# X times its norm weight goes into the layers' projections, and each token's norm factor is multiplied in at the evictions

## The chip, the core and the metric

The kernel runs on one core of a Trainium2 chip. The time is the device time of one execution in microseconds (us). TensorE is the matrix engine (its rows are marked PE, its weight loads PEld), VectorE is DVE, ScalarE is ACT, GpSimd is POOL, and SyncE (SP) issues the transfers. All of them run their own instruction streams in order and wait for each other through semaphores.

## What is computed

512 tokens of width 1024 go through a first block (a time mix, a state space part and a gated feed-forward), a norm, and then two hybrid layers. The end of the first block and the two layers are what the change touches:

```python
x = x + g_f * ffn                                  # end of the first block
x = rms_norm(x) * final_gain
for l in range(2):
    h = rms_norm_2(x, norm_g[l])                   # x * rsqrt(mean(x*x) + 1e-6) * g
    proj = h @ w_in[l]                             # latents, gates, conv, window q/k/v
    y = concat(mla(proj...) * silu(g_mla), conv(proj...) * silu(g_conv), swa(proj...) * silu(g_swa))
    x = x + y @ w_out[l]
```

In `mla`, the query and key-value latents are each normed over their own width before their second projection. The convolution multiplies two projections, filters the product over three tokens and multiplies by a third.

## The kernel before

Everything is held transposed: a tile is 128 features by 512 tokens, and X is eight such tiles. Each float32 product is done in three passes: an operand is split into a rounded high part and the remaining low part, and high times high, high times low and low times high are summed in PSUM. For the activations this split lies in H (`Hs[r]`, a pair for each of the eight row blocks of the input width). For the weights it is made as they arrive: the stream of 234 units of 512 KB each (eight 128x128 blocks) is loaded by SyncE into a ring of four, ScalarE writes the high part (L2151) and VectorE the low part (L1260). Each engine's program calls `blocks(n)` as TensorE consumes blocks, and at each new unit `ahead` puts the split of the next one into that engine's stream. The high and low parts have two places each, so a split waits until TensorE is done with the unit two before it.

All matmuls of one kind are issued by one helper (L394), all transposes by another (L397); VectorE's two-tensor operations are L1260, its scalar-tensor-tensor operations L1268, its copies L1271; ScalarE's activations are L2148 and its copies L2151; GpSimd's are L2790 and L2793. So rows are told apart by tiles, shapes and order.

PSUM banks are handed out in turn: `take` gives the bank that was freed longest ago and waits for the events that empty it; `give` puts it back with those events.

A layer starts with a norm. While the down projection (for layer 0) or the out projection (for layer 1) runs, VectorE adds each finished tile into X, ScalarE squares it and VectorE adds up the squares. After the last tile, TensorE sums the squares over the partitions (`token_sums`, one column per 128 tokens), VectorE and ScalarE make the reciprocal root of the mean for each token, VectorE writes it onto a diagonal (`diag`), and TensorE spreads it over all partitions by a product with ones (`spread`). For layer 0 two norms follow each other, the first block's last one (`f`) and the layer's own (`g`); the second is worked out from sums of squares that carry the first one's weight, so both spreads are made before any row. The two diagonals share one place in memory. Then VectorE makes the rows (`norm_two_rows`, `norm_apply`): X times weight times spread, for layer 0 first X itself and then the row. ScalarE copies the row as high part, and VectorE or GpSimd (in turn) subtracts for the low part. `dense_rows` multiplies row by row with the four latent tiles (three of 128 and one of 32 columns), so each row starts when its H is ready.

The latents are squared and copied by ScalarE, summed over the partitions by TensorE (24 matmuls of one column), and a small part is transposed. Then three stages follow, in which parts of several generators are woven by a fixed pattern, the same on all engines: `qk` (queries and keys by 128 tokens) with the gate tiles 4 to 7 of the projection, `heads` (scores, exponentials, products with V for eight heads) with the window's queries, keys, values and its gates (30 to 33) and the first convolution tiles, and `windows` (four windows of 128 tokens, in two rounds each of `windows` to one of the projection) with the rest of the convolution tiles. For each j of 0 to 3 the projection's order is 8+j, 16+j, 12+j, 20+j. Before, ScalarE copied 8+j to CH; VectorE multiplied 16+j with it into CU; GpSimd and VectorE applied the three taps; VectorE multiplied by 12+j; ScalarE copied 20+j to the gate tile. The round of windows 2 and 3 on VectorE is: tile 8+3, maxima of window 2, 16+3, scores of window 3, 12+3, maxima of window 3, 20+3. Softmax of a window needs VectorE's maxima, ScalarE's eight exponentials, VectorE's reciprocal and GpSimd's product, and only then TensorE's transposes.

## Time and profile before

| | |
|---|---|
| median of 3 runs | 1645.88 us (1645.59 to 1646.56) |
| the profiled execution | 1645.37 us, its span 1643.6 us |
| TensorE busy | 1492.7 us (91%) |
| VectorE busy | 805.6 us (49%) |
| ScalarE busy | 584.4 us (36%) |
| GpSimd busy | 269.5 us (16%) |
| mean granted TensorE clock | 0.959 |

The span is what the trace covers; the execution's time is 1.8 us longer. A granted clock of 1.00 is 2.4 GHz and 0.50 is 1.2 GHz. A row of the timeline gives the start, the duration, the engine, the line and operation, the output and inputs with their shapes, how many instructions are merged in it, and in brackets the idle time of that engine before it and who ended it. With merged instructions the duration is that of the whole group.

### The profile page before, as it was taken

The numbers are of one execution on the slowest core, as the hardware profiler recorded it, in microseconds if no ns is written. First come the engines' busy times: TensorE is split into PE (matmuls) and PEld (weight loads), VectorE is DVE, ScalarE is ACT, GpSimd is POOL, SyncE is SP. The second block draws the span as 40 slices with busy tenths as digits, with TensorE's granted clock in tenths as the row PEclk, the third lists the DMA queues.
The fourth block names the chain that finished last, engine by engine and source line by source line (L and its number), as shares of the span: only waits on it lengthen the run. The fifth ranks groups of instructions, "written<-read, shape, count | busy, mean of one in ns | idle before, by whom it ended". The sixth has DMA issues, their size and how long they took to land.

```text
span 1643.6 us, 23774 instructions
## 1 busy us (share of the span) xinstructions
PE 1492.7 (91%) x10032; PEld 1155.1 (70%) x10032; DVE 805.6 (49%) x1255; ACT 584.4 (36%) x1012; POOL 269.5 (16%) x225
## 2 busy tenths in 40 slices
PE   6998897987899999999988999988898899998899
PEld 3676675875688888888766777666676677766667
DVE  7766855245543323223445554356534655435652
ACT  4265231245333222322333434134523343323441
POOL 0000232001001101100012332222101233222210
PEclk9999999998899999999989999999998999999999
DMA  9258242521222232332311121201222112120121
GB/s 376 71 116 109 70 171 106 165 83 44 72 90 90 90 103 90 104 121 92 119 47 39 52 77 53 76 26 52 72 95 84 39 52 78 51 77 26 52 90 64
DMA packets 51369, 143.12 MB, mean 87 GB/s; under 512 B 13248, under 2 KB 17984, under 8 KB 50496
## 3 DMA queue, kind: packets, MB, share of 16 engines
q1 hardware_dynamic: 51264, 141.60, 27.2%
q8 instruction: 80, 1.31, 0.3%
q14 instruction: 25, 0.20, 0.0%
HBM read 136.90 MB, written 4.69 MB: 86 GB/s over the span
## 4 chain that ended last, share of the span: by engine, by line
PE 72%; DVE 12%; ACT 8%; issue 3%; POOL 1%; DMA 1%; SPq 1%; DVEq 0%; ACTq 0%
PE b L394 71%; ACT arena L2148 5%; DVE arena L1260 2%; DVE ring L1260 2%; DVE arena L1268 2%; PE b L397 1%; ACT ring L2151 1%; POOL arena L2793 1%; DVE arena L1978 1%; ACT L2148 1%; ACT arena L2151 1%; DVE X L1260 1%; DVE arena L2111 1%; ACT tile L2151 1%; DVE arena L1936 1%
## 5 line engine op out<-in xcount | busy, mean ns | idle before, releaser
L394 PE MATMUL b<-tile,ring 128*128 128x512 f32 x2288 | 702.4, 401 | 14.8 <-ACT tile L2151 7.7
L394 PE MATMUL b<-HR,ring 128*128 128x512 f32 (+1 forms) x1888 | 625.1, 407 | 62.9 <-DVE ring L1260 34.9
L394 PEld LDWEIGHTS b<-tile,ring 128*128 128x128 f32 x2288 | 435.1, 191 | 122.4 <-issue 14.3
L394 PEld LDWEIGHTS b<-HR,ring 128*128 128x128 f32 (+1 forms) x1888 | 363.1, 192 | 163.9 <-issue 61.6
L1260 DVE TENSOR_TENSOR ring<-ring,ring 128x1024 fp32r<-128x1024 f32 x186 | 254.8, 1372 | 298.6 <-ACT ring L2151 294.8
L2151 ACT ACTIVATE ring<-ring 128x1024 fp32r<-128x1024 f32 x186 | 195.6, 1054 | 210.2 <-PE b L394 210.2
L394 PE MATMUL b<-arena 64*64 64x64 f32 (+10 forms) x3104 | 232.2, 286 | 26.4 <-issue 9.7
L394 PEld LDWEIGHTS b<-arena 64*64 64x64 f32 (+5 forms) x3104 | 149.3, 149 | 98.1 <-issue 70.6
L1260 DVE TENSOR_TENSOR arena<-arena 128x512 f32<-128x512 f32 (+7 forms) x206 | 110.7, 569 | 74.8 <-ACT arena L2148 53.7
L2151 ACT ACTIVATE arena<-b 128x512 f32<-128x512 f32 (+2 forms) x146 | 78.2, 559 | 193.2 <-PE b L394 153.2
L2793 POOL TENSOR_SCALAR arena<-arena 128x128 f32<-128x128 f32 (+1 forms) x64 | 87.1, 1377 | 209.0 <-DVE arena L1983 209.0
L2790 POOL TENSOR_TENSOR tile<-arena,tile 128x512 fp32r<-128x512 f32 x38 | 51.1, 1351 | 427.9 <-ACT tile L2151 427.9
L2790 POOL TENSOR_TENSOR arena<-arena 128x256 f32<-128x256 f32 (+4 forms) x61 | 65.0, 1089 | 236.0 <-DVE arena L2120 88.3
L1260 DVE TENSOR_TENSOR arena<-b,arena 128x512 f32<-128x512 f32 (+3 forms) x78 | 47.8, 630 | 109.7 <-PE b L394 108.4
L2148 ACT ACTIVATE arena<-arena 128x256 f32<-128x256 f32 (+5 forms) x155 | 73.0, 493 | 78.2 <-DVE arena L1264 46.0
L2148 ACT ACTIVATE arena<-b,arena 128x512 f32<-128x512 f32 (+1 forms) x80 | 44.0, 559 | 112.7 <-DVE arena L1264 108.4
L2151 ACT ACTIVATE tile<-arena 128x512 fp32r<-128x512 f32 x58 | 35.2, 628 | 134.3 <-DVE arena L1260 115.4
L397 PEld LDWEIGHTS b<-cst,arena 128*128 128x128 f32 (+1 forms) x504 | 57.1, 138 | 19.7 <-issue 14.8
L397 PE MATMUL b<-cst,arena 128*128 128x128 f32 (+1 forms) x504 | 63.4, 276 | 7.8 <-POOL arena L2790 5.7
L394 PE MATMUL b<-ring,HR 128*128 128x512 f32 (+1 forms) x256 | 64.5, 344 | 1.7 <-DVE arena L1271 1.2
L2148 ACT ACTIVATE arena<-b,par 128x512 f32<-128x512 f32 (+1 forms) x62 | 40.3, 686 | 65.7 <-PE b L394 38.8
L2148 ACT ACTIVATE arena<-b 128x512 f32<-128x512 f32 (+1 forms) x44 | 24.7, 562 | 84.6 <-PE b L394 84.6
(117 smaller groups left out, 985.7 us busy)
## 6 DMA issues: line engine op xcount, KB each, us to landing
ring<-in_ws SPq DMA_DIRECT2D x218, 512.0 KB, 3.5
arena<-in_ws SPq DMA_DIRECT2D x15, 512.0 KB, 15.3
arena<-in_lw SPq DMA_DIRECT2D x2, 1280.0 KB, 5.5
X<-in_xT SPq DMA_DIRECT2D x2, 1024.0 KB, 6.3
arena<-scr_kpad SPq DMA_DIRECT2D x8, 256.0 KB, 11.5
X<-in_xT SPq DMA_DIRECT2D x1, 2048.0 KB, 8.0
outT<-X SPq DMA_DIRECT2D x8, 256.0 KB, 2.0
arena<-in_cst SPq DMA_DIRECT2D x1, 1088.0 KB, 5.0
```

The lines of the kernel that those rows point to most:

```text
L394: return self.e.matmul(out, lhsT, rhs, start=start, stop=stop, skip_group_check=True)
L397: return self.e.transpose(out, in_, self.k.C("ident"))
L1260: return self.e.tensor_tensor(out=out, in0=a, in1=b, op=op)
L1268: return self.e.scalar_tensor_tensor(out=out, in0=a, scalar=s, in1=b, op0=op0, op1=op1)
L1936: self.e.tensor_reduce(out=s_, in_=sq, op=ALU.add, axis=AX.X).then_inc(*dve.inc((l, "sums", q)))
L1978: self.e.tensor_reduce(out=mx[:, q:q + 1], in_=ps[:, o:o + n], op=ALU.max, axis=AX.X).then_inc(*dve.inc((l, "max", h, q)))
L2111: self.e.tensor_reduce(out=mx, in_=Z[:, :, lo:256], op=ALU.max, axis=AX.X).then_inc(*dve.inc((l, "wmax", n)))
L2148: return self.e.activation(out, a, f, scale=scale, **kw)
L2151: return self.e.activation(out, a, ACT.Copy)
L2790: return self.e.tensor_tensor(out=out, in0=a, in1=b, op=op)
L2793: return self.e.tensor_scalar(out=out, in0=a, scalar1=s1, scalar2=None, op0=op0)
```

## The change

H is no longer the normed row. For both layers it is X times the norm weight (for layer 0 times the product of both weights), without the token's factor, and is made tile by tile while the projection before it runs: `high` on ScalarE, `lower` on VectorE, all eight rows. GpSimd makes no low part of H any more. TensorE's latents follow the projection before them; `token_sums` comes between rows 3 and 4 and `spread` after row 7. The statistics are made on VectorE and ScalarE beside rows 4 to 7 (`token_factors`), and ScalarE copies the spreads to memory (`factors`). The latents are left unscaled, since their own norms take the factor out again if 1e-6 is divided by its square (`e2`). Everything else is multiplied by the factor as it is evicted: gate tiles and 8+j on VectorE instead of copies on ScalarE, the product with 16+j and that with 12+j by one further VectorE multiply each, the window's queries, keys and values by a per-token scalar in the evictions they had. The residual X of layer 0 gets the first block's last norm by eight VectorE products (`residual`), two after each of the gate tiles 4 to 7.

The diff, cut to its core (TensorE, then VectorE, then ScalarE):

```diff
@@ TensorE: latents, and its callers
-        self.norm_two()
         for l in range(2):
-            if l == 1:
-                self.norm("l1")
             self.layer(l)
...
+        self.dense_rows(tiles, ready, M, range(4))
+        for name in names:
+            self.token_sums(name)
+            self.give((name, "sums"), (nd, (name, "mean")))
+        self.dense_rows(tiles, ready, M, range(4, 8))
+        for name in names:
+            self.spread(name)
+            self.give((name, "spread"), (na, (name, "R")))
@@ VectorE
+    def lower(self, name, r, gain):
+        self.wait_ge(k.s("norm_act"), (name, "hi", r))
+        hi, lo = k.Hs[r]
+        self.stt(lo, k.Xk[r], gain, hi.bitcast(F32), ALU.mult, ALU.subtract).then_inc(*k.s("norm_dve").inc((name, "lo", r)))
...
+        if not l:
...
+            self.diag("f", "h2", r_)
+            self.wait_ge(act, ("g", "sqrt"))
+            self.e.reciprocal(r2, r2).then_inc(*dve.inc(("g", "root")))
+            self.wait_ge(dve, ("g", "root"))
+            self.tt(r2, r2, r_, ALU.mult).then_inc(*dve.inc(("g", "both")))
+            rt = r2
...
+        self.diag("l1" if l else "g", "g" if l else "f", rt)
+
+    def residual(self, r):
...
+        self.stt(X, X, k.pc("fgain", r), k.RF, ALU.mult, ALU.mult).then_inc(*k.s("norm_dve").inc(("f", "x", r)))
@@ VectorE, the end of the first block
             if n:
+                self.lower("g", n - 1, k.gg[:, n - 1:n])
                 self.add_square("f", n - 1)
                 self.add_square("g", n - 1)
         self.add_square("f", 7)
         self.add_square("g", 7)
+        self.lower("g", 7, k.gg[:, 7:8])
@@ VectorE, latents
-        self.dense_tiles(4, self.norm_apply("l1", [k.pc("ng1", r) for r in range(8)]) if l else self.norm_two_rows())
+        self.ahead()
+        for r in range(8):
+            self.blocks(4)
+            if r == 4:
+                self.token_factors(l)
@@ VectorE, dense_rest
+        def scaled(m, dst, event):
+            self.wait_ge(D, (name, m))
+            self.wait_ge(k.s("norm_act"), ("l1" if l else "g", "R"))
+            self.tt(dst, k.bank[name, m][:, :], k.RR, ALU.mult).then_inc(*dve.inc(event))
         for n in range(4):
             self.blocks(8)
+            scaled(4 + n, k.G[:, n, :], (l, "g", n))
+            if not l:
+                self.residual(2 * n)
+                self.residual(2 * n + 1)
             yield
...
         for j in range(4):
             self.blocks(8)
+            scaled(8 + j, k.CH, (l, "ch", j))
             yield
...
-            self.tt(CU[:, 2:514], k.bank[name, 16 + j][:, :], k.CH, ALU.mult).then_inc(*dve.inc((l, "cu", j)))
+            self.tt(CU[:, 2:514], k.bank[name, 16 + j][:, :], k.CH, ALU.mult).then_inc(*dve.inc((l, "cr", j)))
+            self.wait_ge(dve, (l, "cr", j))
+            self.tt(CU[:, 2:514], CU[:, 2:514], k.RR, ALU.mult).then_inc(*dve.inc((l, "cu", j)))
...
-            self.tt(y, y, k.bank[name, 12 + j][:, :], ALU.mult).then_inc(*dve.inc((l, "yc", j)))
+            self.tt(y, y, k.bank[name, 12 + j][:, :], ALU.mult).then_inc(*dve.inc((l, "yr", j)))
+            self.wait_ge(dve, (l, "yr", j))
+            self.tt(y, y, k.RR, ALU.mult).then_inc(*dve.inc((l, "yc", j)))
             yield
             self.blocks(8)
+            scaled(20 + j, k.G[:, 4 + j, :], (l, "g", 4 + j))
             yield
@@ ScalarE
+    def high(self, name, r, gain, *when):
...
+        self.af(k.Hs[r][0], k.Xk[r], ACT.Copy, scale=gain).then_inc(*k.s("norm_act").inc((name, "hi", r)))
+
+    def factors(self, name, dst):
...
+        self.wait_ge(k.s("norm_pe"), (name, "spread"))
+        self.cp(dst, k.bank[name, "spread"][:, :]).then_inc(*k.s("norm_act").inc((name, "R")))
@@ ScalarE, latents
+        if not l:
+            self.factors("f", k.RF)
+        self.factors("l1" if l else "g", k.RR)
         for n in range(3):
             ps = k.bank[name, n]
             self.wait_ge(D, (name, n))
```

## Rows read from the trace of the kernel before

**Rows 1.** The page's chain of work that ended last, share of the span by engine

```profile
PE 72%; DVE 12%; ACT 8%; issue 3%; POOL 1%; DMA 1%; SPq 1%; DVEq 0%; ACTq 0%
```

**Rows 2.** Windows: from:to, length, busy time of each engine, granted clock, DMA share

```profile
815.90:830.50 14.60, 6.39 (x32) 5.82 (x33) 9.03 (x18) 3.23 (x6) 2.14 (x4) 0.64 0.31 112
857.20:863.50 6.30, 6.30 (x15) 3.29 (x14) 0.30 (x2) 2.04 (x5) 0.61 (x1) 0.73 0.00 0
1269.00:1273.60 4.60, 4.60 (x15) 2.58 (x14) 0.31 (x2) 2.04 (x5) 0.61 (x1) 1.00 0.01 4
1082.80:1168.60 85.80, 71.94 (x332) 51.73 (x333) 53.01 (x72) 39.36 (x106) 19.89 (x9) 0.92 0.12 37
```

**Rows 3.** Timeline of TensorE at both layers' first projections

```profile
818.57 2.31 PE L394 MATMUL b<-cst,arena 128*128 128x1 f32 x16 [2.74 <-DVE arena L1260]
...
822.45 2.04 PE L394 MATMUL b<-nst,cst 128*128 128x128 f32 x8 [1.58 <-DVE nst L1416]
...
830.52 0.76 PE L394 MATMUL b<-HR,ring 128*128 128x512 f32 x1 [3.10 <-DVE tile L1260]
...
835.01 0.40 PE L394 MATMUL b<-tile,ring 128*128 128x512 f32 x1
...
837.79 0.39 PE L394 MATMUL b<-tile,ring 128*128 128x512 f32 x1
...
854.19 2.73 PE L394 MATMUL b<-cst,arena 128*128 128x1 f32 x24
...
1241.28 0.77 PE L394 MATMUL b<-HR,ring 128*128 128x512 f32 x1 [2.32 <-DVE tile L1260]
...
1265.98 2.73 PE L394 MATMUL b<-cst,arena 128*128 128x1 f32 x24
```

**Rows 4.** Timeline of VectorE at the same two boundaries

```profile
815.87 0.75 DVE L1268 SCALAR_TENSOR_TENSOR X<-b,ada,X 128x512 f32<-128x512 f32 x1 [3.23 <-PE b L394]
816.54 2.49 DVE L1260 TENSOR_TENSOR arena<-arena 128x512 f32<-128x512 f32 x4
818.94 1.22 DVE L1260 TENSOR_TENSOR ring<-ring,ring 128x1024 fp32r<-128x1024 f32 x1
...
1231.80 0.69 DVE L1260 TENSOR_TENSOR X<-b,X 128x512 f32<-128x512 f32 x1 [3.22 <-PE b L394]
```

**Rows 5.** Timeline of ScalarE, the first of the latents' squares in layer 0

```profile
852.31 0.60 ACT L2148 ACTIVATE arena<-b 128x512 f32<-128x512 f32 x1 [2.35 <-PE b L394]
```

**Rows 6.** Timelines of VectorE and TensorE in layer 0's query-key stage

```profile
873.22 1.75 DVE L1936 TENSOR_REDUCE arena<-arena 128x16 f32<-128x1536 f32 x1 [0.29 <-ACT arena L2148]
...
913.09 1.43 DVE L1264 TENSOR_SCALAR arena<-b,par 96x512 f32<-96x512 f32 x2
...
915.15 2.40 PE L394 MATMUL b<-arena 96*128 96x512 f32 x8 [0.97 <-ACT arena L2148]
```

**Rows 7.** TensorE's wait in layer 0's heads; VectorE's groups by shape, 1280 to 1640 us

```profile
1051.86 0.61 PE L394 MATMUL b<-HR,ring 128*128 128x512 f32 x1 [3.06 <-DVE ring L1260]
...
L1271 DVE COPY arena<-b 128x512 f32<-128x512 f32 x20 | 13.3, 679 | 6.8 <-PE b L394 6.6 <-PE b L397 0.2
...
L1260 DVE TENSOR_TENSOR arena<-b,arena 128x512 f32<-128x512 f32 x7 | 4.8, 681 | 7.4 <-PE b L394 7.4
```

**Rows 8.** Timelines of all engines in layer 0's window stage

```profile
1116.69 0.76 PE L394 MATMUL b<-HR,ring 128*128 128x512 f32 x1 [5.54 <-DVE ring L1260]
...
1119.99 2.27 DVE L2111 TENSOR_REDUCE arena<-arena 128x8 f32<-128x2048 f32 x1
...
1124.24 0.60 ACT L2151 ACTIVATE arena<-b 128x512 f32<-128x512 f32 x1 [9.57 <-PE b L394]
...
1129.39 3.61 POOL L2790 TENSOR_TENSOR arena<-arena 128x2048 f32<-128x2048 f32 x1 [13.93 <-DVE arena L2120]
...
1130.82 3.25 DVE L1260 TENSOR_TENSOR ring<-ring,ring 128x1024 fp32r<-128x1024 f32 x1 [0.35 <-ACT ring L2151]
...
1153.09 2.37 PE L397 MATMUL b<-cst,arena 128*128 128x128 f32 x16 [2.83 <-POOL arena L2790]
```

More of the change, by code:

```diff
@@ L1008, in latents @@
         pe, act, dve = k.s("lat_pe"), k.s("lat_act"), k.s("lat_dve")
[L1009 to L1012 removed]
+        na, nd = k.s("norm_act"), k.s("norm_dve")
+        names = ("l1",) if l else ("f", "g")
+        ready = [[(na, (names[-1], "hi", r)), (nd, (names[-1], "lo", r))] for r in range(8)]
+        tiles, M = [(self.name, n) for n in range(4)], [128, 128, 128, 32]
+        self.dense_rows(tiles, ready, M, range(4))
[6 more added lines that the diff above has]
+            self.give((name, "spread"), (na, (name, "R")))
         for n in range(3):
@@ L2031, in gate @@
             self.blocks(8)
[L2032 to L2033 removed]
+            scaled(30 + n, k.G[:, 8 + n, :], (l, "g", 8 + n))
         for n, _ in enumerate(self.window_norm(l)):
@@ L2583, in latents @@
         name = f"l{l}"
-        self.dense_tiles(4, self.norm_apply("l1") if l else self.norm_two_rows())
+        self.ahead()
+        for r in range(8):
+            self.blocks(4)
+            if r == 4 and l:
+                self.norm_root("l1", k.r_)
+            elif r == 4:
+                self.norm_root("f", k.r_)
+                self.norm_root("g", k.r2_)
+        if not l:
+            self.factors("f", k.RF)
+        self.factors("l1" if l else "g", k.RR)
         for n in range(3):
@@ L2704, in dense_rest @@
         for j in range(4):
-            self.blocks(8)
-            self.wait_ge(dve, (l, "cu", j - 1) if j else (l, "pad"))
-            copy(8 + j, k.CH, (l, "ch", j))
-            yield
-            self.blocks(8)
-            yield
-            self.blocks(8)
-            yield
-            self.blocks(8)
-            copy(20 + j, k.G[:, 4 + j, :], (l, "g", 4 + j))
-            yield
+            for _ in range(4):
+                self.blocks(8)
+                yield
         self.gates(l, range(4, 8))
```

186 lines of the change are left out of this document (81 added, 105 removed).

## The prediction, made before the changed kernel had run

> **What bounds the kernel now.** I read the chain that ended last first: 72% of it is TensorE and 12% VectorE [rows 1], so time is to be had only where TensorE stands still. Then the timeline of TensorE around the two layers' first projections. Between the last matmul of the down projection and the first of layer 0's latents lie 14.6 us, in which only small matmuls (column sums, spreads) run and the granted clock averages 0.64 [rows 2, 3]: TensorE waits for sums, roots, the spread, and then for the first row of H. In layer 1 the same gap is 9.5 us, from the last eviction into X to the first latent matmul [rows 3, 4]. That is what the change attacks. Third, I read what VectorE does where TensorE waits later in a layer, because the change moves work there: the stage with the window attention (1082.8 to 1168.6 us) has TensorE busy for 71.9 of 85.8 us [rows 2], and its waits end with a VectorE weight split or with a GpSimd product that VectorE started [rows 8]. VectorE has 53.0 us of work there, but it is a queue with long waits in it, so added work counts whenever it stands ahead of a split that TensorE wants.
>
> **The boundary.** The split of X times its weight is made per tile while the down (or out) projection runs, so the latents' rows 0 to 3 can follow at once. Twelve matmuls of 512 columns take 2.78 us (835.01 to 837.79), 96 take 22.2. The sums stay on TensorE, now between rows 3 and 4: 2.3 us for both in layer 0 [rows 3], half of that (1.0) in layer 1, with one. Does the second weight unit come in time? VectorE has after the last down tile: eviction 0.75, then four adds at 0.62 each, then the split 1.22, which began at 818.94 [rows 4]. Two more products (0.67 each) put it at 820.3, ready at 821.6; TensorE wants it 5.55 us after 815.9, at 821.4: 0.2 us lost. Layer 0's rows then end at 815.9 + 22.2 + 2.3 + 0.2 = 840.6 instead of 854.2; layer 1's at 1231.8 + 23.2 = 1255.0 instead of 1266.0 [rows 3, 4]. But the spreads now stand behind the rows and in front of the evictions: one took 2.04 us at the 1.2 GHz level [rows 3], so about 1.0 at 2.4 GHz. In layer 0: spread, the second diagonal on VectorE (0.69; it shares its memory with the first, so it waits), spread, and ScalarE's copy before the latents' squares (0.5; the squares are alike [rows 5]), with hand-overs 3.5 us; in layer 1 one spread and one copy, 1.6 us. Before, the first square began at 852.31, 1.9 us ahead of the rows' end [rows 5], because tile 0 was finished first. That lead is lost. So the first square starts at 844.1 instead of 852.3 (-8.2) and at 1256.6 instead of 1264.1 (-7.5). The 24 one-column matmuls behind it ran 2.73 us after the rows; now they follow each square and end 0.9 us after the third, which is 0.8 us sooner against the squares. Together **-9.0 and -8.3 us**. The statistics' own chain (root, reciprocals, four more tiny ones) lies under rows 4 to 7, 11 us.
>
> **The clock.** The stretch of one-column matmuls and the first product after it took 4.6 us at full clock in layer 1, and 6.3 us at 0.73 in layer 0 [rows 2]: the same work, and one of two such stretches cost 1.7 us. Afterwards each stretch holds more idle time (waits for diagonal, copy, squares), and layer 0 has one more in the middle of its rows, the sums. Bounds: nothing, and three falls (5.1 us). I take one and a half, **+2.6 us**, since layer 1's becomes emptier than the one that fell.
>
> **Query-key stage.** The gate tiles' evictions move from ScalarE (which waited for TensorE there anyway, so it frees nothing) to VectorE, in layer 0 with two residual products each: 0.65 + 2 x 0.75 us (the eviction into X has that form [rows 4]). Before the second reduction VectorE is idle 0.29 us in layer 0 [rows 6], and the other layer runs alike. That reduction sets when a bank is free for the next projection, so +1.8 and +0.35 us. The third and fourth reductions have over 3 us of idle time before them, which hides it. At the end of the stage the last group stands ahead of the transposed keys' eviction (913.09), and the scores wait at 915.15 for ScalarE, 0.7 us later than VectorE [rows 6]: +1.7 and +0.15. Together **+4.0**. If a slow clock falls on this stage, TensorE is late and hides 1.8 of it; that is the lower bound, 1.1 us for both layers with the rest.
>
> **Heads.** Evictions that only change from copy to product cost nothing I can find: a copy 128x512 out of PSUM takes 0.68 us and a product 0.68 [rows 7]. New are two products with the spread per convolution tile. Two of them lie ahead of a chain that ends in a split TensorE waits for: the wait of 3.06 us at 1051.86 [rows 7] is such a chain (product, GpSimd tap, two taps, masks, exponentials, split), +0.7 (a product and its hand-over). One round earlier such a chain shows no wait yet; it can cost from nothing to 0.7, and as the two rounds are alike but for a tap I take 0.5. Both layers: **+2.4**, bounds 0 and 3.
>
> **Windows.** Here a wait is added. At 1119.99 VectorE begins the maxima of window 2, while TensorE still runs projection tile 8+3, begun at 1116.69. The product that evicts this tile now comes first in VectorE's queue and waits for its end; behind it stand the maxima, the exponentials that depend on them, the reciprocal, GpSimd's product and the next weight splits. ScalarE had the same wait, for its copy at 1124.24, so the exponentials began half a us later, at 1124.7 [rows 8]. Step by step: the product on y before window 1 shifts all by 0.7. Eviction done at 1125.4, maxima 2.3 and small ones 0.5, exponentials from about 1128.2: +3.4. The split behind them lasts until GpSimd's product of 3.61 us ends (it took 3.25 us at 1130.82, 1.22 at 818.94 [rows 4, 8]). TensorE's tile 12+3 then starts 2.2 us late, 20+3 3 us late. Two more products (+1.35) stand before the exponentials of window 3; those are 4.7 us late, GpSimd's last product too, and for that TensorE waits at 1153.09 [rows 8]. So +4.6 per layer, **+9.2**. Bounds: 1.4 (only the first product counts) and 13 (each longer wait also lowers the clock).
>
> On that hold: splits beside a GpSimd product took 3.25 us against 1.22 alone [rows 4, 8]. The Trainium skill (SBUF — State Buffer, Who interferes with whom) says that a VectorE instruction with two SBUF inputs and a GpSimd instruction that reads SBUF exclude each other, the loser waiting for the whole instruction. By that rule the products with the spread, which have two SBUF inputs, would be held where GpSimd scales probabilities; I find none of these on TensorE's path, so the sum would stay.
>
> **Sum.** -17.3 + 2.6 + 4.0 + 2.4 + 9.2 = +0.9 us. The profiled execution took 1645.37 us (span 1643.6 and 1.8 around it), the median of the runs is 1645.88, 0.5 above it. 1645.9 + 0.9 = 1646.8 us.
>
> **Rivals.** *Faster:* the boundary pays and most of the later work stays hidden. That is so if VectorE's wait for tile 8+3 costs little (windows +1.4 a layer, 2.8) and the clock does not fall anew: -17.3 + 4.0 + 2.4 + 2.8 = -8, 1638 us. For it: VectorE is busy only 53.0 of 85.8 us in the worst stage. Against it: the queue order, which idle time elsewhere doesn't mend.
> *Slower:* the wait for tile 8+3, in the window stage, is the mechanism. It makes TensorE stand for 4.4 us instead of 2.8 ahead of 1153.09 and for 1.5 and 0.9 us at two tiles that had no wait. If these lower the clock once more in each layer (1.7 us each, as above) and the boundary's stretches fall all three times (+2.5 on my figure), it is +0.9 + 3.4 + 2.5 = +6.8, 1652.7 us. It decides from about 6 us a layer on, where my sum has 4.6.
> *The rows don't start at once:* if the first rows wait for the last tile's split (a unit or a bank not ready), some 5 us of each gap return: 1656 us. Against it: rows 0 to 3 need only tiles finished long before.
>
> **How the numbers follow.** A measurement of this kernel can tell 0.2% (3.3 us) from no change. Forecast 0.45, faster rival 0.24, slower 0.27, rows late 0.04. The forecast's own range is 1642.5 to 1650; the range that leaves out no more than 2 in 10 is 1639 to 1653. Of the forecast's chance nearly all lies within 0.2%; a little of each rival does too. So faster 0.24, same 0.46, slower 0.30.
>
> **What would show it.** Right: the first latent matmul within 0.3 us of the last down matmul and rows ending 24.7 us later; the first square 28 and 25 us after that boundary in layers 0 and 1; VectorE idle until the end of tile 8+3, with the maxima behind it, and the wait for GpSimd near 4.4 us; 4.6 us more from the first window score to the out projection. Wrong: if the stretch from the first latent product to the out projection is not longer by some 6 to 9 us a layer, the gain of the boundary stays and the kernel is faster; if rows 0 to 3 show waits for splits, the boundary's gain was too large.

## The result and the profile after

The changed kernel takes 1660.19 us (median of four runs, 1656.38 to 1665.68), the kernel before beside it 1646.22. The ratio is 1.0087, interval 1.0054 to 1.012: **slower**, by 14 us, where the forecast was 1646.8. The profiled execution is the quickest of the four, 1656.38 us (span 1654.6). The four runs differ by 9 us, and from the quickest to the slowest their mean granted clocks are 0.959, 0.958, 0.951 and 0.948. The four of the kernel before lie within 1.5 us of each other. One of the 17 runs of the kernel before that stood beside e9 to e12 below took 1898.4 us at a granted clock of 0.739 and enters none of the ratios and means.

First the new boundary, TensorE's timeline (start, duration, engine, line, operation, count, and in brackets the idle time before it with what ended it). These lines answer to [rows 3]:

```profile
822.09 0.47 PE L396 MATMUL b<-HR,ring 128*128 128x512 f32 x1 [0.22 <-issue]
...
827.72 1.84 PE L396 MATMUL b<-cst,arena 128*128 128x1 f32 x16
...
842.44 1.16 PE L396 MATMUL b<-nst,cst 128*128 128x128 f32 x8 [0.78 <-DVE nst L1255]
...
844.77 3.58 PE L396 MATMUL b<-cst,arena 128*128 128x1 f32 x24 [1.17 <-ACT arena L2182]
```

and the first of the latents' squares on ScalarE, which answers to [rows 5]:

```profile
844.13 0.59 ACT L2182 ACTIVATE arena<-b 128x512 f32<-128x512 f32 x1
```

The rows follow the down projection at once, with 0.22 us lost for the second weight unit (VectorE's split of it begins at 820.77 and takes 1.22 us). The column sums take 1.84 us in the middle. The first square starts at 844.13, where I had 844.1, and 8.2 us earlier than before [rows 5]. The boundary did what it should.

Then TensorE's waits in layer 0, where the change added work to VectorE. They answer to [rows 6, 7, 8]:

```profile
871.27 0.80 PE L396 MATMUL b<-HR,ring 128*128 128x512 f32 x1 [3.62 <-DVE arena L1255]
...
911.62 4.00 PE L396 MATMUL b<-arena 96*128 96x512 f32 x8 [1.76 <-DVE arena L1259]
...
1026.13 0.47 PE L396 MATMUL b<-HR,ring 128*128 128x512 f32 x1 [0.54 <-DVE ring L1255]
...
1052.55 0.76 PE L396 MATMUL b<-HR,ring 128*128 128x512 f32 x1 [3.78 <-DVE ring L1255]
...
1118.36 0.79 PE L396 MATMUL b<-HR,ring 128*128 128x512 f32 x1 [5.21 <-DVE arena L1255]
...
1139.55 0.47 PE L396 MATMUL b<-HR,ring 128*128 128x512 f32 x1 [1.66 <-DVE ring L1255]
...
1147.65 0.47 PE L396 MATMUL b<-HR,ring 128*128 128x512 f32 x1 [0.56 <-DVE ring L1255]
...
1159.88 3.65 PE L399 MATMUL b<-cst,arena 128*128 128x128 f32 x16 [4.57 <-POOL arena L2829]
```

Nearly every stall has the size that was forecast: 0.54 and 0.72 more in the heads (I had 0.5 and 0.7), 1.66 at tile 12+3 (1.5), 0.56 at tile 20+3 (0.9), 4.57 for GpSimd's last product (4.4). Only the one at 1118.36 is of another kind: it ends with a VectorE product that frees a bank (arena), and in [rows 8] it ended with a weight split (ring). The queues behind it, VectorE and then GpSimd:

```profile
1113.48 4.22 DVE L1255 TENSOR_TENSOR ring<-ring,ring 128x1024 fp32r<-128x1024 f32 x1 [0.54 <-ACT ring L2185]
1117.63 0.68 DVE L1255 TENSOR_TENSOR arena<-b,nst 128x512 f32<-128x512 f32 x1
...
1126.73 0.69 DVE L1255 TENSOR_TENSOR arena<-b,nst 128x512 f32<-128x512 f32 x1 [4.91 <-PE b L396]
1127.34 2.28 DVE L2145 TENSOR_REDUCE arena<-arena 128x8 f32<-128x2048 f32 x1
```

```profile
1113.02 3.60 POOL L2829 TENSOR_TENSOR arena<-arena 128x2048 f32<-128x2048 f32 x1 [12.22 <-DVE arena L2154]
1134.72 3.60 POOL L2829 TENSOR_TENSOR arena<-arena 128x2048 f32<-128x2048 f32 x1 [18.10 <-DVE arena L2154]
```

At 1126.73 stands the wait of the forecast: 4.91 us idle, the eviction of tile 8+3, and only then the maxima of window 2, which in [rows 8] began at 1119.99. At 1117.63 stands what I had missed: the eviction of tile 20+2 is behind a split of 4.22 us, and its bank is the one that tile 8+3 needs. The split began while GpSimd's product of 3.60 us was running and ended 1.08 us after it. The kernel before has this long split too, but there ScalarE evicted tile 20+2:

```profile
1112.32 4.22 DVE L1260 TENSOR_TENSOR ring<-ring,ring 128x1024 fp32r<-128x1024 f32 x1 [0.55 <-ACT ring L2151]
```

The Trainium skill (SBUF — State Buffer, Who interferes with whom) gives the rule for this pair, that the later one waits for the whole instruction; the trace agrees, with 1.22 us for the same split elsewhere [rows 4].

So where do 14 us come from? The stretches, cut at the same events in both profiles (last eviction of the down projection, first scores, last heads' products, first output rows past their split, and the same in layer 1):

| stretch | before, us | after, us | difference | forecast (without clock) |
|---|---|---|---|---|
| layer 0, boundary and query-key | 99.28 | 95.25 | -4.0 | -5.5 |
| layer 0, heads | 167.71 | 171.88 | +4.2 | +1.2 |
| layer 0, windows | 85.75 | 93.19 | +7.4 | +4.6 |
| output, boundary, query-key of layer 1 | 156.64 | 148.77 | -7.9 | -7.8 |
| layer 1, heads | 167.68 | 170.49 | +2.8 | +1.2 |
| layer 1, windows | 85.58 | 93.58 | +8.0 | +4.6 |
| sum of these | 762.64 | 773.16 | +10.5 | -1.7 |

The forecast's clock term of +2.6 lay in the first and fourth line. The same stretches of the changed kernel by windows (from:to, length, busy time and count of TensorE, its weight loads, VectorE, ScalarE, GpSimd, then granted clock, DMA share, GB/s); the third answers to the last of [rows 2]:

```profile
816.37:841.50 25.13, 24.91 (x120) 18.47 (x118) 10.26 (x21) 6.40 (x9) 3.15 (x4) 1.00 0.32 108
...
911.62:1083.50 171.88, 160.93 (x740) 123.15 (x741) 87.17 (x158) 55.68 (x116) 49.92 (x37) 0.97 0.19 62
1083.50:1176.69 93.19, 75.18 (x333) 54.67 (x333) 56.95 (x78) 37.81 (x103) 19.89 (x9) 0.89 0.10 34
...
1325.46:1495.95 170.49, 159.46 (x741) 122.29 (x741) 86.99 (x158) 56.39 (x116) 49.84 (x37) 0.98 0.19 64
1495.95:1589.53 93.58, 74.12 (x333) 53.66 (x333) 56.94 (x78) 37.81 (x103) 19.89 (x9) 0.89 0.11 34
```

The heads' 740 matmuls keep TensorE busy for 160.93 us; before it was 157.83 with the same count, at 0.99:

```profile
915.15:1082.86 167.71, 157.83 (x740) 121.19 (x741) 80.15 (x148) 58.41 (x119) 51.63 (x37) 0.99 0.19 65
```

The window stage has 75.18 against 71.94 [rows 2]. That is not waiting but slower work: the clock. Over the heads and windows of both layers TensorE's busy time grew by 8.9 us. Where it lies in the changed kernel, and where it lay before:

```profile
977.00:982.00 5.00, 5.00 (x16) 3.92 (x15) 3.01 (x3) 0.00 (x0) 4.13 (x3) 0.66 0.46 147
1103.00:1107.00 4.00, 4.00 (x12) 3.14 (x11) 3.97 (x6) 0.00 (x0) 0.00 (x0) 0.57 0.33 125
1117.00:1125.00 8.00, 6.64 (x18) 5.26 (x19) 4.83 (x7) 0.00 (x0) 0.00 (x0) 0.57 0.42 133
1158.00:1166.00 8.00, 6.12 (x26) 4.21 (x28) 4.71 (x4) 3.00 (x5) 1.74 (x1) 0.57 0.20 66
```

```profile
819.00:834.00 15.00, 9.44 (x39) 8.12 (x39) 8.66 (x18) 2.30 (x5) 3.43 (x5) 0.54 0.17 66
1236.00:1247.00 11.00, 7.77 (x22) 5.89 (x23) 6.64 (x10) 3.16 (x5) 2.51 (x2) 0.53 0.20 65
```

In a window with clock c, 2(1-c) of its length was at 1.2 GHz. Summed over windows of 1 us, the kernel before has 23.8 us at that level in its two boundaries, where TensorE had little to do, and 48.9 us in the rest of the two layers. The changed kernel has none in the boundaries and 78.4 us in the rest, nearly all of it next to waits of 1.8 to 6.8 us or to the squares behind the new boundary. Not every wait there is new: the low stretch at 977 follows a wait of 2.56 us that the kernel before has as well, without a fall. The two sums for the whole execution hardly differ (134 and 136 us). In the front part, which the change doesn't touch, each profile has 51 to 72 us, as it comes.

Two theories, then. **Queues:** what VectorE's order costs, some 11 us in the windows instead of 9.2, is the loss, and the clock is chance. **Clock:** the new stalls bring falls of the clock, onto busy matmuls. And within the second, either the falls follow the stalls, or an execution has its 136 us at 1.2 GHz whatever is done and the old boundary merely hid 24 of them.

### The profile page after: what moved, and what is told of

Its sections match the earlier page's. It is cut to its first block, busy times and chain, and to the rows that moved or that the text cites. A ratio compares the mean times of both kernels' runs of the same rounds, so it can differ in the third digit from the quotient of the medians.

```text
span 1654.6 us, 23782 instructions
## 1 busy us (share of the span) xinstructions
PE 1497.2 (90%) x10032; PEld 1157.4 (70%) x10032; DVE 823.9 (50%) x1297; ACT 573.9 (35%) x993; POOL 256.8 (16%) x217
## 4 chain that ended last, share of the span: by engine, by line
PE 70%; DVE 14%; ACT 7%; issue 4%; POOL 3%; DMA 1%; SPq 1%; DVEq 0%; ACTq 0%
PE b L396 69%; ACT arena L2182 4%; DVE arena L1255 3%; DVE arena L1263 2%; DVE ring L1255 1%; PE b L399 1%; DVE arena L1998 1%; ACT ring L2185 1%; POOL arena L2832 1%; POOL arena L2829 1%; DVE arena L2145 1%; DVE arena L1956 1%; DVE arena L1259 1%; DVE X L1255 1%; DMA arena<-scr_yd 1%
## 5 line engine op out<-in xcount | busy, mean ns | idle before, releaser
L396 PE MATMUL b<-arena 64*64 64x64 f32 (+10 forms) x3104 | 236.8, 287 | 28.8 <-issue 11.5
L2832 POOL TENSOR_SCALAR arena<-arena 128x128 f32<-128x128 f32 (+1 forms) x64 | 83.6, 1322 | 214.8 <-DVE arena L2003 214.8
L2185 ACT ACTIVATE arena<-b 128x512 f32<-128x512 f32 (+2 forms) x113 | 61.2, 563 | 97.4 <-PE b L396 58.6
L396 PE MATMUL b<-ring,HR 128*128 128x512 f32 (+1 forms) x256 | 64.8, 345 | 1.4 <-DVE arena L1266 1.2
L2182 ACT ACTIVATE arena<-b 128x512 f32<-128x512 f32 (+1 forms) x44 | 24.7, 562 | 115.6 <-PE b L396 115.6
```

The costliest lines, as they stand in the source:

```text
L396: return self.e.matmul(out, lhsT, rhs, start=start, stop=stop, skip_group_check=True)
L2182: return self.e.activation(out, a, f, scale=scale, **kw)
L2185: return self.e.activation(out, a, ACT.Copy)
L2832: return self.e.tensor_scalar(out=out, in0=a, scalar1=s1, scalar2=None, op0=op0)
```

## The experiments

All are compared with the kernel before, run beside them on the same chip (medians 1648.56, 1651.03 and 1650.34 us in the three groups, each on another chip, 1642.8 to 1656 in single runs). "At 1.2 GHz" is 2(1-clock) times the span, mean over the runs. Within each kernel's own runs, a microsecond more at that level goes with 0.31 us more time (all kernels pooled; 0.17 to 0.46 in single ones).

| run | what | median, us | ratio [95%] | at 1.2 GHz, us |
|---|---|---|---|---|
| kernel before (three groups) | | 1648.6 to 1651.0 | 1 | 138 to 142 |
| e5_after_again | the changed kernel | 1663.42 | 1.0088 [1.0069, 1.0106] | 163 |
| e1_no_factor | changed kernel, leaves the token factor out of gates and convolution | 1638.90 | 0.9936 [0.9919, 0.9953] | 133 |
| e2_late_ch | tile 8+3 evicted behind the maxima | 1652.37 | 1.0016 [1.0002, 1.003] | 142 |
| e3_no_second | changed kernel, leaves the second products out | 1647.17 | 0.9990 [0.9978, 1.0003] | 131 |
| e4_before_dve_evicts | kernel before, evictions on VectorE | 1659.61 | 1.0066 [1.0047, 1.0085] | 149 |
| e6_reordered | changed kernel, same work elsewhere | 1633.79 | 0.9913 [0.9896, 0.9930] | 120 |
| e7_after_filled | changed kernel, waits filled | 1647.98 | 0.9995 [0.9983, 1.0007] | 91 |
| e11_fill_one | changed kernel, one wait filled | 1653.17 | 1.0017 [1.0002, 1.0033] | 133 |
| e12_after_all_filled | e7 with one fill moved and one added | 1636.66 | 0.9921 [0.9900, 0.9941] | 78 |
| e8_before_filled | kernel before, boundary waits filled | 1643.08 | 0.9962 [0.9949, 0.9975] | 113 |
| e10_before_all_filled | kernel before, boundary and layer waits filled | 1629.36 | 0.9875 [0.9846, 0.9904] | 71 |
| e9_reordered_filled | e6, waits filled | 1621.12 | 0.9812 [0.9787, 0.9838] | 75 |

### The changed kernel again

> The changed kernel itself, beside the others on one chip. If the 9 us between its four runs are the clock's own spread, its median lies at 1656 to 1662 and its ratio to the kernel before at 1.005 to 1.009; put at the same time at 1.2 GHz as the kernel before (some 0.3 us of time for each us at that level), it stays 7 to 8 us above it, which is the part that the queues cost.

It came out at 1663.42 us, above the expected 1656 to 1662, and at 1.0088, within the expected ratios, with 163 us at 1.2 GHz. Over its ten runs on two occasions the mean is 159 us, against some 140 for the kernel before. At 0.31 us each these 19 us are 5.9 us of the 14 (with this group's runs alone, 24 us and 7.5); the other 7 to 8 are there at equal time at 1.2 GHz. They are not the queues' alone, since a microsecond at that level does not cost the same everywhere: in the profiles heads and windows have some 23 us more of it and 9 us of time with it, while the 24 us of the old boundary are worth 4.8 us (e8, below). The profiled run had been a favourable one.

### The boundary alone

```diff
-            scaled(8 + j, k.CH, (l, "ch", j))
...
-            self.tt(CU[:, 2:514], k.bank[name, 16 + j][:, :], k.CH, ALU.mult).then_inc(*dve.inc((l, "cr", j)))
-            self.wait_ge(dve, (l, "cr", j))
-            self.tt(CU[:, 2:514], CU[:, 2:514], k.RR, ALU.mult).then_inc(*dve.inc((l, "cu", j)))
+            self.tt(CU[:, 2:514], k.bank[name, 16 + j][:, :], k.CH, ALU.mult).then_inc(*dve.inc((l, "cu", j)))
...
-            scaled(20 + j, k.G[:, 4 + j, :], (l, "g", 4 + j))
```

with ScalarE's copies of gates 4 to 7, 8+j and 20+j put back.

> The changed kernel with its new boundary kept (split ahead of the statistics, sums after row 3, spreads behind the rows, the residual products), but without the token factor in the gate and convolution tiles: gates 4 to 7, 8+j and 20+j are copied by ScalarE again as before, and the second products on the convolution input and on y are gone. It leaves out the factor of these tiles, so its time is that of less work on VectorE. Queue theory: the stalls of TensorE that VectorE's longer queue makes go, 0.35 us of the query-key stage, 1.2 of the heads and 5.3 of the windows in each layer, 13.8 us in all: 1656.4 - 13.8 = 1642.6. Two forms of the clock theory stand beside it. If the falls of the clock on busy matmuls come from the new stalls, another 5 us go and it takes 1637 to 1638, with less than 125 us at the 1.2 GHz level. If the whole execution holds some 136 us at that level whatever is done, and the old boundary only took 24 of them while TensorE had little to do, they stay on busy matmuls and it takes 1642 to 1643.

1638.90 us: ten microseconds (0.9936) under the kernel before, below what the queues give (1642.6) and next to the first form of the clock theory (1637 to 1638), though with 133 us at 1.2 GHz and not under 125. The window stages are back at their old length:

```profile
913.45:1082.46 169.01, 159.40 (x740) 122.31 (x741) 80.32 (x148) 58.13 (x121) 51.72 (x37) 0.98 0.19 63
1082.46:1167.72 85.26, 73.09 (x332) 53.27 (x333) 52.95 (x72) 39.36 (x106) 19.86 (x9) 0.92 0.11 38
```

So the boundary's gain is real and was kept; all of the loss is brought by the factor's work in the layers. And against the changed kernel's ten runs 26 us at 1.2 GHz went, which the queue theory doesn't give.

### The evictions alone, in the kernel before

```diff
-            self.proj(l, 8 + j, (act, (l, "ch", j)))
+            self.proj(l, 8 + j, (dve, (l, "ch", j)))
...
+            copied(8 + j, k.CH, (l, "ch", j))
```

and so for gates 4 to 7 and 20+j.

> The kernel before, with one thing of the change: ScalarE's copies of gates 4 to 7, of tiles 8+j and of 20+j are made by VectorE, at the places where the change has its products. No factor, no second products, boundary as before; everything is computed. Queue theory: the wait for tile 8+3 ahead of the maxima and the bank that now comes free behind the long split cost 3.3 + 0.7 us in the windows of each layer and up to 0.5 us in its query-key stage: +8 to +9 us over the kernel before, 1654 to 1655. If new stalls bring falls of the clock, 3 to 5 us more: 1657 to 1660. If ScalarE's copy was as late as VectorE's product, and the place costs nothing: 1646 to 1648.

1659.61 us, +11, the upper case. TensorE's timeline in the window stage, and that stage:

```profile
1117.25 0.65 PE L394 MATMUL b<-HR,ring 128*128 128x512 f32 x1 [3.50 <-DVE arena L1271]
...
1137.48 0.47 PE L394 MATMUL b<-HR,ring 128*128 128x512 f32 x1 [1.66 <-DVE ring L1260]
```

```profile
1082.86:1171.72 88.86, 74.44 (x333) 54.21 (x333) 54.82 (x75) 37.81 (x103) 19.86 (x9) 0.90 0.11 36
```

The wait that frees a bank is there with a plain copy too, and the stall of 1.66 at tile 12+3 is the same to the hundredth. The stage grows by 3.1 us, and by 3.3 in layer 1: that is the price of the place, without the factor. It is not the queue's alone, as TensorE's busy time in it grew from 71.94 to 74.44 us. The two stretches with the query-key stages grow by another 1.8 and 0.8 us in this profile. Over its runs this kernel has 11 us more at 1.2 GHz than the kernel before, at 0.31 us each 3.4 of the 11 us. How much of the rest is waiting is not shown.

### One product moved, and the second products left out

```diff
             self.blocks(8)
-            scaled(8 + j, k.CH, (l, "ch", j))
+            if j not in (3,):
+                scaled(8 + j, k.CH, (l, "ch", j))
             yield
             self.blocks(8)
+            if j in (3,):
+                scaled(8 + j, k.CH, (l, "ch", j))
```

> The changed kernel with one product moved: the eviction of tile 8+3 stands behind the maxima of window 2 in VectorE's queue, no longer ahead of them. Everything is computed. Queue theory: the maxima start when they did before the change, so the delays of 2.2 us at tile 12+3 (1.66 of stall), 0.56 at 20+3 and most of the 1.8 us that GpSimd's last product is late go; the longer wait at tile 8+3 (5.2 us, of which some 1.4 to 2 come from the products ahead of the split) stays. 2.5 to 3.5 us a layer, 5 to 7 in all: 1649.5 to 1651.5. If the falls of the clock come from the stalls, 2 to 3 us more and below 1649. If the wait for tile 8+3 is not what delays the exponentials, it stays at 1655 to 1657.

> The changed kernel without the eight second products a layer pair of the convolution tiles: the factor is left out of the convolution input once and of y, so each convolution tile has two products fewer on VectorE. Waits and order are as in the changed kernel. Queue theory: the 0.54 and 0.72 us in the heads go, 0.7 us before window 1's split, and 0.7 of the delay ahead of window 3's exponentials: 2.4 to 2.9 us a layer, 5 to 6 in all, so 1650.5 to 1651.5, and the stalls of 1.66 and 0.56 us at tiles 12+3 and 20+3 stay at 1 us or more. If only the clock costs, the time does not follow the products and stays within 2 us of 1656.

```profile
1085.96:1175.09 89.13, 74.72 (x333) 54.65 (x333) 56.99 (x78) 37.94 (x103) 19.87 (x9) 0.90 0.11 36
```

```profile
1084.13:1172.77 88.64, 71.65 (x332) 52.17 (x333) 54.84 (x75) 37.81 (x103) 19.86 (x9) 0.92 0.11 36
```

(the first of e2_late_ch, the second of e3_no_second.) They take 4.1 and 4.6 us off the window stage of 93.19. In the first the stalls before tiles 12+3 and 20+3 are gone, as expected, and GpSimd's last product is waited for 3.33 us. In the second 1.66 stays and GpSimd's is 2.62; the stall before tile 20+3, expected to stay, is gone too. Both kernels are faster than expected as a whole: they lie 12 and 16 us under the changed kernel by the ratios, where the queues alone give 5 to 7. The time at 1.2 GHz is 16 and 28 us lower, worth 5 and 9 us. The stalls removed are small in time, and more time came back than they had taken.

### The same work in other places

```diff
+        self.tt(k.RR2, k.RR, k.RR, ALU.mult).then_inc(*dve.inc((l, "rr2")))
...
+            self.tt(k.CH, k.bank[name, 8 + j][:, :], k.RR2, ALU.mult).then_inc(*dve.inc((l, "ch", j)))
...
+        self.mid = {1: lambda: (last(2), scaled(22, k.G[:, 6, :], (l, "g", 6))),
+                    2: lambda: halve(3), 3: lambda: last(3)}
...
             self.tt(es, sink, mx, ALU.subtract).then_inc(*dve.inc((l, "es", n)))
+            if n in self.mid:
+                self.mid[n]()
             self.wait_ge(act, (l, "es", n))
```

`last(j)` is the product of y with the factor row; the residual products stand between the heads.

> The changed kernel with the same work in other places, everything computed. Layer 0's residual products stand between the heads, no longer in the query-key stage. The square of the factor row is made once, and the first product of each convolution tile uses it, so one of the two second products is gone. The other second product of tiles 2 and 3, the eviction of tile 20+2 and that of tile 8+3 stand in VectorE's wait for the exponentials of windows 1, 2 and 3. Queue theory: 3.5 us of layer 0's query-key stage, 1.2 us of the heads and 5.3 of the windows in each layer come back, 16.5 us: 8 to 9 us under the kernel before, ratio 0.994 to 0.996, with the stall before tile 12+3 gone and the one for GpSimd's last product at 2.8 us instead of 4.6. If the costs are the clock's and not the queue's, it stays within 3 us of the changed kernel.

1633.79 us, 0.9913 where 0.994 to 0.996 was expected: 14 us faster than the kernel before by the ratio (17 by the medians) and nearly 30 faster than the changed one, with all the work of the change but one product less per tile. VectorE in the window stage:

```profile
1116.37 0.16 DVE L1255 TENSOR_TENSOR arena<-par,arena 128x8 f32<-128x8 f32 x1
1118.06 0.69 DVE L1255 TENSOR_TENSOR arena<-b,arena 128x512 f32<-128x512 f32 x1 [1.54 <-PE b L396]
1120.68 0.17 DVE L1255 TENSOR_TENSOR arena<-arena 128x8 f32<-128x8 f32 x1 [1.92 <-ACT arena L2202]
```

Tile 8+3 is evicted at 1118.06 inside the 4.2 us in which VectorE waits for the exponentials anyway, and adds no wait. With 20+2 evicted before the long split, TensorE's wait at tile 8+3 ends with a weight split again, as in [rows 8], and the one for GpSimd's last product is 2.61 us (expected 2.8):

```profile
1110.48 0.77 PE L396 MATMUL b<-HR,ring 128*128 128x512 f32 x1 [5.53 <-DVE ring L1255]
...
1146.75 1.94 PE L399 MATMUL b<-cst,arena 128*128 128x128 f32 x16 [2.61 <-POOL arena L2849]
```

The two following stretches of layer 0, heads and windows:

```profile
909.28:1076.60 167.32, 157.72 (x740) 121.32 (x741) 91.13 (x164) 56.34 (x116) 50.79 (x37) 0.99 0.19 65
1076.60:1161.85 85.25, 70.45 (x333) 51.37 (x333) 56.03 (x77) 37.92 (x103) 19.86 (x9) 0.94 0.12 38
```

Both have their old length (167.71 and 85.75). The queue theory's 16.5 us are there, and 12 more. It has 39 us less at 1.2 GHz than the changed kernel's ten runs; times 0.31 that is those 12.

### Waits filled with idle matmuls

```diff
+    def fill(self, n):
+        k = self.k
+        for _ in range(n):
+            self.mm(k.banks[7][:, :], k.Hs[0][0][:, 0:128], k.Hs[0][0], True, True)
...
     def proj(self, l, n, *emptied):
         k = self.k
+        self.fill({5: 12, 6: 7, 7: 7, 32: 8, 21: 13, 22: 9, 11: 19, 15: 5}.get(n, 0))
         ps = self.take((self.name, n))
```

Nobody reads bank 7 then. The other waits have the same line ahead of them.

> The changed kernel, everything computed, with matmuls whose results nobody reads put ahead of TensorE's longest waits in both layers (3 before the column sums of the latents, 12, 7 and 7 before gate tiles 5 to 7, 4 before the first scores, 8 before tile 32, 13 before 20+1, 9 before 20+2, 19 before 8+3, 5 before 12+3, 9 before the last head's product, 16 before the last window's transposes), each 0.24 us and together somewhat shorter than the wait. Same queues, same waits, TensorE busy in them. If the falls of the clock come from the stalls, those in the layers mostly go: some 30 us less at 1.2 GHz and 5 to 9 us less time, 1648 to 1651. If the time at 1.2 GHz does not depend on the waits, it stays the same as the changed kernel or becomes up to 3 us longer.

> The changed kernel as in e7, with 9 idle matmuls more before the product of head 6 and 11 before the third output tile, two waits that e7 left empty and behind which the clock fell. Ratio 0.996 to 0.999 (e7: 0.9995). Beside e10: equal within 3 us if the change is neutral but for the clock.

> The changed kernel, everything computed, with 19 idle matmuls of 0.24 us at one place, ahead of tile 8+3 in each layer (waits of 5.2 and 6.8 us). If a stall costs by the fall behind it, the 1.2 GHz stretches next to this wait (6.8 and 10.2 us in the two layers) go and the others stay: 3 to 5 us less than the changed kernel, ratio 1.004 to 1.006. If the falls just move to another place, it stays at 1.008 to 1.009.

The fills of e7 take the changed kernel from 1.0088 to 0.9995, and those of e12 to 0.9921 (expected 0.996 to 0.999), though no other engine's queue was changed and TensorE has more to do. The second step is not all clock: the time at 1.2 GHz went from 91 to 78 us, at 0.31 us each 4 of its 12 us. In e7 the 9 matmuls "before the last head's product" (head 7) filled no wait. They stand in the middle of a run of busy matmuls, and TensorE's wait of 2.76 us just ahead, for head 6, stayed empty; e12 moved them there (its expectation speaks of 9 more) and added the 11 before the third output tile. The first rows are e7's, the second e12's:

```profile
1080.63 3.79 PE L396 MATMUL b<-arena 128*64 128x512 f32 x8 [2.76 <-DVE arena L1286]
1084.35 2.36 PE L396 MATMUL b<-HR 128*128 128x512 f32 x9
```

```profile
1078.62 2.33 PE L396 MATMUL b<-HR 128*128 128x512 f32 x9
1081.63 5.76 PE L396 MATMUL b<-arena 128*64 128x512 f32 x32 [0.68 <-DVE arena L1288]
```

So e7 carries some 5 us of added matmuls in its two layers (2.36 and 2.90) that e12 has not, and e12 is the one to go by. Filling one wait per layer gives 1.0017, three quarters of e7's step and more than I expected. Its 20 us around that wait, and the same stretch of the changed kernel (two us earlier there):

```profile
1115.00:1135.00 20.00, 20.00 (x96) 15.56 (x94) 12.82 (x16) 7.57 (x24) 4.17 (x2) 1.00 0.16 54
```

```profile
1113.00:1133.00 20.00, 14.79 (x62) 12.05 (x62) 11.64 (x12) 5.30 (x16) 3.60 (x1) 0.83 0.17 54
```

The fall at this wait is gone. Layer 0 as a whole still has 44.4 us at 1.2 GHz in this execution (44.3 in the changed kernel), since the low stretches at 1052 and 1103 are longer and one at 888 is new; layer 1 went from 34.1 to 24.9. So falls follow waits, but which of the waits brings one, and for how long, differs from run to run, and only the medians tell.

In the kernel before, with 512-column matmuls of constants in the waits of both boundaries:

> The kernel before, everything computed, with idle matmuls of the same kind (0.55 us each at 2.4 GHz) in the waits of its two boundaries only: 4 ahead of the sums, 2 and 1 ahead of the spreads and 5 ahead of the first row in layer 0, 4, 2 and 3 in layer 1. The boundary stays as long as it is. If the falls come from the idle time, the 24 us at 1.2 GHz in the two boundaries go, and with them 2 to 4 us of time (the column sums, the spreads and the first product behind them run at 2.4 GHz): 1643 to 1645, ratio 0.997 to 0.999. If an execution has its 136 us at that level whatever TensorE does in the boundary, they move to busy matmuls: 4 to 7 us longer, 1650 to 1653.

```profile
819.43:833.40 13.97, 13.96 (x57) 7.80 (x56) 10.10 (x19) 3.23 (x6) 2.14 (x4) 1.00 0.34 117
1231.60:1241.00 9.40, 9.40 (x35) 5.08 (x34) 6.43 (x10) 2.41 (x4) 2.59 (x4) 1.00 0.55 197
```

1643.08 us, 0.9962 (expected 0.997 to 0.999): the clock is 1.00 where it was 0.54 and 0.53, and the 24 us did not move to the layers (52 us in the rest of them, 49 before). Over the runs the time at 1.2 GHz fell from 139 to 113 us. That decides between the two forms: **the falls follow the stalls; there is no fixed amount.** It does not say that each stall brings a fall. It also shows that the old boundary's low clock had its price, 6 us of time by the ratio and 8 by the medians. In the profile the two stretches with the boundaries are 3.8 and 1.0 us shorter.

### Both kernels with the clock held up

> The kernel before, everything computed, with idle matmuls at the same places of its layers and in its two boundaries (as in e8). It tells what the change is worth where the clock hardly falls in either kernel. e8 took 0.9962; with the layers' stalls filled too, another 25 to 30 us at 1.2 GHz go: ratio 0.988 to 0.991. If my sum without its clock term is right (-17.3 + 4.0 + 2.4 + 9.2 and 1.4 for the bank that comes free late, about 0), the filled kernel before and the filled changed kernel (e12) lie within 3 us of each other. If the queues cost more than that, the changed one is 6 to 8 us behind.

> The reordered kernel (e6) with idle matmuls of 0.24 us ahead of TensorE's waits in both layers (3 before the latents' column sums, 8, 7 and 7 before gate tiles 5 to 7, 3 before the first scores, 8 before tile 32, 10 before 20+1, 9 before 20+2, 14 before 8+3, 9 before the product of head 6, 9 before the last window's transposes, 11 before the third output tile). Everything is computed. The reordered kernel has some 40 us at 1.2 GHz in its layers; if the falls come from the stalls, they go to 10 or less, at 0.28 us of time for each, 8 to 9 us: ratio to the kernel before 0.985 to 0.987. If what is left falls anyway, 0.990 to 0.993.

Both came out faster than expected (0.9875 against 0.988 to 0.991, 0.9812 against 0.985 to 0.987). Heads and windows of layer 1, where the kernels run at 1.00; first the kernel before, then the changed one, then the windows alone of the reordered one:

```profile
1316.97:1483.01 166.04, 162.49 (x767) 124.80 (x768) 80.14 (x148) 58.36 (x119) 51.57 (x37) 1.00 0.20 66
1483.01:1565.27 82.26, 77.03 (x373) 56.88 (x373) 52.95 (x72) 39.37 (x106) 19.90 (x9) 1.00 0.12 39
```

```profile
1318.41:1485.76 167.35, 163.24 (x770) 125.32 (x771) 86.97 (x158) 56.39 (x116) 49.85 (x37) 1.00 0.20 65
1485.76:1573.54 87.78, 82.07 (x393) 60.54 (x393) 56.83 (x78) 37.83 (x103) 19.91 (x9) 1.00 0.12 37
```

```profile
1464.93:1546.96 82.03, 77.67 (x376) 57.42 (x376) 55.92 (x77) 37.94 (x103) 19.91 (x9) 1.00 0.12 39
```

Here the queues' price stands alone: 1.3 us in the heads (I had 1.2) and 5.5 in the windows (I had 4.6). The reordered kernel has none of the second. Summed over the same six stretches as in the table, the profile of the filled changed kernel is 4.0 us longer than that of the filled kernel before; layer 0's windows hold one fall in it, so it is some 2.4 without. The expectation of about 0 had left out that filling also helps the old boundary: e10's two stretches with a boundary are 97.05 and 154.31 us, where they were 99.28 and 156.64. With these 4.6 us the sum (-1.7, and 1.8 for what the windows cost beyond 4.6) would be 4.7, where the stretches show 4.0, or 2.4 without the fall.

The medians differ by 7.3 us (ratios 0.9875 and 0.9921, whose intervals leave 2 to 13 us), so the expected equality within 3 us did not come. The two profiles differ by another 4.3 us ahead of layer 0, where the change does next to nothing; the changed kernel's has 6.9 us more at 1.2 GHz there (71.7 against 64.8), which at 0.31 to 0.5 us each is 2.1 to 3.5 of them. The rest I can't place.

The best kernel of the study is the reordered one with its waits filled, 1621.12 us, 0.9812.

## Why the prediction was wrong

It said 1646.8 (1639 to 1653); the median is 1660.2. The profiled execution is 10.5 us longer in the stretches above, where I had 0.9. The median lies another 3.8 us above the profiled execution.

- **The boundary: right.** Layer 0's rows end 24.2 us after it (I had 24.7), the first squares start 27.8 and 24.5 us after it (28 and 25). With the query-key stages it is -11.9 us in all, against -10.7 with the forecast's clock term. The -17.3 were counted from an old boundary at the low clock; 4.6 to 4.8 of them can be had in the old boundary too, by filling its waits (e10, e8).
- **Query-key stage: right.** The second reduction stands 1.6 us later, counted from the first (I had 1.8), TensorE's wait behind it is 3.62 us and was 2.08, and the scores wait for VectorE. e6 took the residual products away and got the wait down from 3.62 to 2.30 us. The lower bound that was given for this stage, 1.1 us, does not follow from 4.0 less 1.8, which is 2.2.
- **Heads: right as a queue.** 0.54 and 0.72 us, and 1.3 in a kernel whose clock stays up. But the profile shows +4.2 and +2.8, and the 4.6 us beyond 2.4 are low clock on busy matmuls (TensorE's busy time for them grew by 3.1 and 1.6 us).
- **Windows: a term missing.** The chain through tile 8+3 was as told, step for step: the idle VectorE, maxima behind it, 1.66, 0.56, 4.57. I had followed the products that stand ahead of the maxima, but had not asked which bank tile 8+3 takes. That is the bank of 20+2, whose eviction moved from ScalarE to VectorE behind a split of 4.22 us. In the filled kernels, whose clock stays up, tile 8+3 starts 0.66 us after the split's end with the change and 0.14 without, so this costs 0.5 of the 0.9 us by which the windows' 5.5 per layer exceed 4.6; the other 0.4 I can't place. The term that was mis-sized by it is the +9.2, which measured 11.0. Under "evictions that only change from copy to product cost nothing" a place in another queue had been priced as if it were the same one.
- **The clock: the step that failed.** I counted falls only in the boundary, one and a half, +2.6 us. I knew the stalls in the windows, priced a fall at 1.7 us, and gave both of them only to a rival, one fall a layer. What had been put at nothing without a reason is the low clock on the busy matmuls of heads and windows. In the profile it is 9.0 us there (4.6 and 4.4), the largest part of the miss. The median's 3.8 us above the profile go with more time at 1.2 GHz, by the granted clocks of the four runs. Removing or filling stalls gave back more than the queues' share each time: e2, e3, e6, e7, e11, e12.
- **The spread.** I took the 1 us between three runs for the precision of any kernel of this kind. The changed kernel's runs spread over 9 us, and on other occasions those of the kernel before over 12. The range had no room for it.

Of the rivals the slower one named the right mechanism (the wait for tile 8+3, and falls behind it) and had 1652.7; it was too small because it allowed the window stages two more falls, 3.4 us of time, where there are, in the layers, 29 us more at 1.2 GHz in the most favourable run and 51 in the profile of e5_after_again. "Rows late" did not come: 0.22 us.

On the clock the Trainium skill (TensorE: Matmul & The Clock Gate, HAM oscillation — how this bites in real kernels) describes waits inside a loop that bring the slow clock again and again, there for DMA. These runs agree, for waits on VectorE. The same page, under What's actually happening, puts the penalty of the ramp, the slow matmuls before the clock first rises, under 1% of a typical span. No run here measures that ramp alone; the falls at waits inside the kernel cost more: filling such waits gave 1.25% in the kernel before (e10) and 1.7% in the changed one (e12 against e5).

## What to carry to other kernels

A stall of TensorE can have two prices, the wait itself and the slow matmuls after it. In heads and windows of the changed kernel the second was 9.0 us in the profile (and more in the median), the first 13.4. So a change that trades one long idle stretch for many waits of 2 to 5 us in a busy stage has to be costed with the clock in the busy stage, and work that is added to an in-order queue belongs inside a wait that the queue has anyway: evictions on VectorE, the one ahead of the maxima above all, cost 3 to 4 us a layer with their share of low clock (e4, e2), and in the wait behind the maxima nothing that the window stage shows (e6). When an eviction changes its engine, ask for each bank who takes it next, and what stands ahead of the eviction in its new queue.

## What the runs showed of the hardware

- Matmuls whose results nobody reads, put into waits, made every kernel faster: the kernel before by 1.25%, the changed one by 1.7%, the reordered one by 1.0%, although TensorE had more to do (e10, e12 against e5, e9 against e6). Nine of them at a place without a wait took their own 2.4 and 2.9 us (e7).
- The time that a kernel spends at 1.2 GHz is not the same from run to run: for one and the same kernel 128 to 155 us on one chip (clock 0.961 to 0.953, 1642.8 to 1654.9 us). The kernels with more stalls had more of it (149 us in e4, 159 in the changed kernel, beside 138 to 142 in the kernel before).
- A VectorE split that began beside a GpSimd product of 3.60 us took 4.22 us in the kernel before, in the changed kernel and in e6 alike, 1.2 us alone; it matters as soon as an eviction stands behind it.
- The idle time in the old boundary cost more than its length: filling it, with every step of it left in, gave 6 us by the ratio and 8 by the medians.
